# Low-weight products of the two-row weight pieces, issued singly behind 512-column products instead of in runs

## The reference, cut to what matters

```python
x = x + jnp.square(jax.nn.relu(hf @ ffn_w1[layer])) @ ffn_w2[layer]       # hidden width 4096, two layers
...
return (jax.nn.silu(h @ w_gate) * (h @ w_up)) @ w_down                     # swiglu, hidden width 2816
```

## Time and profile before

| | us |
|---|---|
| median of 3 runs (lowest, highest) | 874.14 (873.94, 874.26) |
| the profiled execution, device time | 874.67 |
| its span, first to last instruction | 872.9 |
| TensorE busy in the span | 864.1 (99%) |
| DVE busy | 622.4 (71%) |
| ACT busy | 452.9 (52%) |

### The profile page before, as it was taken

How to read it: one execution, slowest core, us unless ns; L and a number is a source line. 1 busy time by engine, 2 the same in 40 slices (tenths; PEclk the granted TensorE clock), 3 DMA queues, 4 the chain that set the end, 5 groups by cost and what they waited for, 6 DMA issues and landing times.

```text
span 872.9 us, 12188 instructions
## 1 busy us (share of the span) xinstructions
PE 864.1 (99%) x4714; PEld 739.8 (85%) x4714; DVE 622.4 (71%) x783; ACT 452.9 (52%) x619; POOL 80.9 (9%) x115
## 2 busy tenths in 40 slices
PE   9999999999999999999999999999999999999997
PEld 8988888888888988778888888888877888888886
DVE  6899877766666678857666666667775876676675
ACT  5697554433434578745343444465775844434432
POOL 3484110000000020011000000020000200000000
PEclk9999999999999999999999999999999999999999
DMA  9665356565555362376655555556442456555541
GB/s 303 213 215 193 112 179 219 169 212 192 187 189 193 116 191 86 106 250 204 207 192 190 190 191 193 188 182 200 145 146 97 140 178 213 193 191 193 192 145 48
DMA packets 98393, 155.84 MB, mean 179 GB/s; under 512 B 4144, under 2 KB 73421, under 8 KB 98349
## 3 DMA queue, kind: packets, MB, share of 16 engines
q1 hardware_dynamic: 95644, 149.37, 51.0%
q0 software_dynamic: 1648, 5.80, 2.2%
q10 hardware_dynamic: 1056, 0.07, 0.1%
HBM read 153.62 MB, written 1.09 MB: 177 GB/s over the span
## 4 chain that ended last, share of the span: by engine, by line
PE 98%; DMA 1%; DVE 0%; ACT 0%; issue 0%; SPq 0%; DVEq 0%; POOLq 0%; POOL 0%; ACTq 0%
PE psum L2090 21%; PE psum L1984 16%; PE psum L1985 16%; PE psum L1986 16%; PE psum L2096 11%; PE psum L2076 4%; PE psum L2079 2%; PE psum L2591 1%; PE psum L2622 1%; PE psum L2005 1%; PE psum L2268 1%; PE psum L2604 1%; PE psum L2043 1%; PE psum L2048 1%; PE psum L2044 1%; PE psum L2702 1%
## 5 line engine op out<-in xcount | busy, mean ns | idle before, releaser
L1297 DVE TENSOR_TENSOR w_lo<-raw,w_hi 128x2048 fp32r<-128x2048 f32 (+3 forms) x116 | 259.6, 2247 | 79.9 <-ACT w_hi L793 39.1
L2090 PE MATMUL psum<-h_both,w_hi 128*128 128x512 f32 x800 | 190.0, 389 | 0.0
L2090 PEld LDWEIGHTS psum<-h_both,w_hi 128*128 128x128 f32 x800 | 149.3, 188 | 30.4
L775 ACT ACTIVATE w_hi<-raw 128x2048 fp32r<-128x2048 f32 (+2 forms) x71 | 129.6, 1838 | 36.6 <-PE psum L1986 23.6
L1984 PE MATMUL psum<-w_hi,g_hi 128*128 128x512 f32 x368 | 144.6, 393 | 0.0
L1985 PE MATMUL psum<-w_lo,g_hi 128*128 128x512 f32 x368 | 143.7, 390 | 0.0
L1986 PE MATMUL psum<-w_hi,g_lo 128*128 128x512 f32 x368 | 143.3, 389 | 0.0
L793 ACT ACTIVATE w_hi<-raw 128x2048 fp32r<-128x2048 f32 x66 | 125.7, 1911 | 23.9 <-PE psum L1986 23.9
L2096 PEld LDWEIGHTS psum<-h_both,w_lo 128*128 128x128 f32 x800 | 102.7, 191 | 4.0
L968 ACT ACTIVATE g_hi<-g_mul 128x512 fp32r<-128x512 f32 x32 | 20.3, 634 | 162.7 <-DVE g_mul L1612 162.7
L2096 PE MATMUL psum<-h_both,w_lo 128*128 128x256 f32 x800 | 103.9, 283 | 0.0
(11 more groups left out here) (312 smaller groups left out, 1098.5 us busy)
## 6 DMA issues: line engine op xcount, KB each, us to landing
raw<-in_ffn_w SPq DMA_DIRECT2D x64, 1024.0 KB, 5.3
raw<-in_w_qkv SPq DMA_DIRECT2D x12, 1024.0 KB, 5.1
raw<-in_ab_w_in SPq DMA_DIRECT2D x11, 1024.0 KB, 6.5
raw<-in_w_gate SPq DMA_DIRECT2D x11, 1024.0 KB, 5.3
raw<-in_w_up SPq DMA_DIRECT2D x11, 1024.0 KB, 5.4
raw<-in_w_down SPq DMA_DIRECT2D x11, 1024.0 KB, 5.7
raw<-in_ab_w_out SPq DMA_DIRECT2D x4, 1024.0 KB, 4.9
raw<-in_c_w_out SPq DMA_DIRECT2D x4, 1024.0 KB, 6.5
```

Source lines behind the costliest of these rows:

```text
L775: ins = act.activation(dst, src, ACT.Copy)
L1297: ins = dve.tensor_tensor(dst, src, high, ALU.subtract)
L2090: pe.matmul(bank(b + f), wh[:, k, f * P:(f + 1) * P], h_both[:, k, :, :].rearrange("p u s -> p (u s)"), start=k == 0, stop=False, skip_gro ...
```

## The change

Two functions are new, and the last-row handling of `stationary_both` moves into what follows it.

- `stationary_open` does high(0), with the low products of row 1 of an earlier piece between them where one is given, and then high(1) with low(0) between: one 512-column product, one 256-column product, and so on. It leaves its own low(1) open.
- `out_closing` does the 24 products of `out_piece` and puts the 8 open low products of the piece before behind the first 8 of them; the last of the 8 increments `piece_used` for that piece.
- In `ffn`, each first-matrix piece is `stationary_open` and the second-matrix piece after it `out_closing` (15 chunks in each of the two networks). In the gated network, up closes gate and down closes up (9 chunks). The last gate and up pieces stay with `stationary_both`, whose low(0) now also goes between the products of high(1) for the gate piece.

The numbers and sizes of all products, and DVE's, ACT's and SP's programs, are the same.

The helpers `high_at` and `low_at` issue one product of `high` and `low` each. The diff's core:

```diff
                 else:
-                    high(1)
-                    low(0)
+                    for k in range(KB):
+                        high_at(slot, b, 1, k)
+                        low_at(slot, b, 0, k)
                 low(1).then_inc(piece_used, 1)
+
+            def stationary_open(slot, b, slot_before=None, b_before=None):
+
+                for k in range(KB):
+                    high_at(slot, b, 0, k)
+                    if slot_before is not None:
+                        ins = low_at(slot_before, b_before, 1, k)
+                if slot_before is not None:
+                    ins.then_inc(piece_used, 1)
+                for k in range(KB):
+                    high_at(slot, b, 1, k)
+                    low_at(slot, b, 0, k)
+
+            def out_closing(act_of, n_slot, first, slot_before, b_before):
...
+                            for term, (a, w) in enumerate(((a_hi, wh), (a_hi, wl), (a_lo, wh))):
+                                ins = pe.matmul(bank(2 * tb + h), a, w[:, k, cs], start=first and k == 0 and term == 0,
+                                                stop=False)
+                                if left < KB:
+                                    low = low_at(slot_before, b_before, 1, left)
+                                    left += 1
+                                    if left == KB:
+                                        low.then_inc(piece_used, 1)
+                ins.then_inc(piece_used, 1)
...
-                    stationary_both(n % RING, hidden_banks(j + 1))
+                    stationary_open(n % RING, hidden_banks(j + 1))
...
-                    out_piece(hidden_of(j % 3), (n + 1) % RING, isinstance(c, int) and c == 0)
+                    out_closing(hidden_of(j % 3), (n + 1) % RING, isinstance(c, int) and c == 0,
+                                n % RING, hidden_banks(j + 1))
...
+                    stationary_open(n0 % RING, 4)
+                    split(n0 + 1 + 6 * i)
+                    pe.wait_ge(mul_out, hb + c)
+                    stationary_open((n0 + 1) % RING, 6, n0 % RING, 4)
...
-                out_piece(glu_of(j % 2), (n + 2) % RING, isinstance(c, int) and c == 0)
+                out_closing(glu_of(j % 2), (n + 2) % RING, isinstance(c, int) and c == 0, (n + 1) % RING, 6)
```

More of the change, by code:

```diff
@@ L2081, in stationary_half, with high_at, low_at @@
                 return ins
+            def high_at(slot, b, f, k):
+                wh = w_hi[:, slot, :].rearrange("p (k c) -> p k c", k=KB)
+                return pe.matmul(bank(b + f), wh[:, k, f * P:(f + 1) * P],
+                                 h_both[:, k, :, :].rearrange("p u s -> p (u s)"),
+                                 start=k == 0, stop=False, skip_group_check=True)
+            def low_at(slot, b, f, k):
+                wl = w_lo[:, slot, :].rearrange("p (k c) -> p k c", k=KB)
+                return pe.matmul(bank(b + f)[:, 0:S], wl[:, k, f * P:(f + 1) * P], h_hi[:, k, :],
+                                 start=False, stop=k == KB - 1, skip_group_check=True)
             def stationary_both(slot, b, half_done=None):
-                wh = w_hi[:, slot, :].rearrange("p (k c) -> p k c", k=KB)
-                wl = w_lo[:, slot, :].rearrange("p (k c) -> p k c", k=KB)
                 def high(f):
                     for k in range(KB):
-                        pe.matmul(bank(b + f), wh[:, k, f * P:(f + 1) * P],
-                                  h_both[:, k, :, :].rearrange("p u s -> p (u s)"),
-                                  start=k == 0, stop=False, skip_group_check=True)
+                        high_at(slot, b, f, k)
                 def low(f):
                     for k in range(KB):
-                        ins = pe.matmul(bank(b + f)[:, 0:S], wl[:, k, f * P:(f + 1) * P], h_hi[:, k, :],
-                                        start=False, stop=k == KB - 1, skip_group_check=True)
+                        ins = low_at(slot, b, f, k)
                     return ins
@@ L2104, in stationary_both @@
                 else:
-                    high(1)
-                    low(0)
+                    for k in range(KB):
+                        high_at(slot, b, 1, k)
+                        low_at(slot, b, 0, k)
                 low(1).then_inc(piece_used, 1)
+            def stationary_open(slot, b, slot_before=None, b_before=None):
[9 more added lines that the diff above has]
+            def out_closing(act_of, n_slot, first, slot_before, b_before):
+                wh = w_hi[:, n_slot, :].rearrange("p (k c) -> p k c", k=2)
+                wl = w_lo[:, n_slot, :].rearrange("p (k c) -> p k c", k=2)
+                left = 0
+                for tb in range(TB):
+                    for h in range(2):
+                        cs = slice(h * 512, (h + 1) * 512)
+                        for k in range(2):
+                            a_hi, a_lo = act_of(k, tb)
+                            for term, (a, w) in enumerate(((a_hi, wh), (a_hi, wl), (a_lo, wh))):
[7 more added lines that the diff above has]
+                ins.then_inc(piece_used, 1)
             def stationary_seam(slot, t, b, x_at):
@@ L2858, in gate_up @@
                     pe.wait_ge(gate_scaled, c)
[L2859 to L2862, removed]
+                if isinstance(c, int) and c == GC - 1:
+                    stationary_both(n0 % RING, 4)
+                    split(n0 + 1 + 6 * i)
+                    pe.wait_ge(mul_out, hb + c)
+                    stationary_both((n0 + 1) % RING, 6, up_half)
+                else:
+                    stationary_open(n0 % RING, 4)
+                    split(n0 + 1 + 6 * i)
+                    pe.wait_ge(mul_out, hb + c)
+                    stationary_open((n0 + 1) % RING, 6, n0 % RING, 4)
             def glu_of(r):
```

## The result

| | before | changed |
|---|---|---|
| median, us | 874.35 (873.94 to 875.08, 6 runs) | 882.23 (882.08 to 882.93, 6 runs) |
| span of the profiled execution, us | 872.9 | 880.3 |
| TensorE busy in it | 864.1 | 869.9 |

The changed kernel takes 1.009 times as long, 95% interval 1.008 to 1.010: 7.9 us slower, where 4.3 were forecast; 882.23 lies above the forecast's range, which ended at 881.2. All that follows reads the two traces, whose spans differ by 7.4 us.

A forecast was written before the change was run, and what follows sets the result against it. TensorE, busy 99% of the span, was taken to bound the kernel. Product distances +1.4, two seams +3.0 and the gated network 0 gave +4.4 us; forecast 878.4 us, range 873.6 to 881.2.

The forecast's parts named there:

- the price of a pair: TensorE, one 256-column product behind one 512-column product, repeated: +2 ns each time, 776 times, 1.55 us.
- the products' own part: TensorE's product distances: 1.55 us for alternating sizes, less 0.18 for fewer run exits in gated chunks, +1.4 us.
- The equal 13.3 ns: TensorE: 512- and 256-column products each pay 13.3 ns besides their columns, so no load time is left to hide.
- The two stretches of the earlier trace: TensorE, 384 and 288 columns in turn, two pairs each: 0.62 and 0.63 us against 0.613, +3 to +8 ns a pair.
- The upper bound of 8 ns: TensorE, worst pair of 384 and 288 columns, taken as the most a 512-256 pair could add: +8 ns.
- Seams: After each network's last chunk, DVE's read-out comes 1.82 us later and TensorE's transposes wait: 1.5 us each, +3.0 us.
- The loops: Network and gated chunks: DVE's read-outs come 1.82 us later, yet weights reach TensorE in time; 0 us counted.
- Gaining pairs (1 and 2): TensorE, low behind high cheaper: 6 to 7 ns gained, 873.4 us, chance 0.15; or 9 ns, 872.2, chance 0.05.
- An unstalled seam (3): After each network's last chunk, unseen slack prevents the stall: 875.5 us, or 874.0 with flat pairs; chance 0.12.
- DVE's loop (4): Gated network: DVE's chain to the next up weights binds, each chunk 0.1 to 0.3 longer, 879.5 to 881.5; chance 0.12.
- Pairs at the upper bound (5): TensorE, each high-low pair costs +8 ns: 883.1 us; chance 0.04.
- The signs written down for a wrong forecast: TensorE's timeline: pairs at 0.34 us or less, transposes following at once, or idle before second-matrix or up pieces.

The follow-up runs named there:

- experiment 6: Changed kernel with each low product taking 512 columns instead of 256, so sizes no longer alternate but weights and banks do: 961.79 us.
- experiment 7: Kernel before with each low product right behind its own high one, same bank, lows widened to 384 columns, then 496: 920.77 and 952.11 us.
- experiment 3: Kernel before with row 1's 8 lows in one run behind the second matrix's first 8 products, all 15 chunks of each network: 878.14 us.
- experiments 1 and 2: Changed kernel, each network's last first-matrix piece closing itself: 879.78 us; kernel before, last chunks' 8 row-1 lows put behind 8 second-matrix products: 877.33 us.
- experiment 5: Kernel before with the bank changing at every product while the sizes stay in runs of 16 highs, then 16 lows: 874.39 us.

## Why the prediction was wrong

**The step that failed is the price of a pair,** the 2 ns in "What does one low behind one high cost, repeated?". It measured 6.7 ns: 776 x 6.7 = 5.2 us in place of 1.55. With the exits, the products' own part came to 5.0 us where 1.4 was forecast; the 0.18 that the gated chunks were to gain by one exit less did not come. The equal 13.3 ns of long and short products was read rightly, and nothing speaks against the conclusion that no load time is there to be hidden: in experiment 6 the loads still come from `w_hi` and `w_lo` in turn, at no cost, and in experiment 7 a low that gives a load more time is no cheaper. The mistake came behind it. The two stretches of the earlier trace rows gave +3 and +8 ns as they are printed, and the value taken lay below both, for a reason (the mixed sizes around them) for which there was no row. Their middle, 5.5, would have given 881.2, the upper end of the range. But the rows themselves could not have given 6.7: to the nanosecond they are 616 and 624 ns, +1.3 and +5.3 a pair, and each holds only two pairs, less than the three after which the pattern of 512 and 256 repeats. The upper bound of 8 ns held by the rounding of the rows, a piece of luck; a chance of 0.04 was all that it got, and so the range ended below it.

**Seams: right, a little large.** 2.5 us in place of 3.0. The chain was the one described, each step behind the other. Its 0.5 us too much hid a part of the pairs' miss in the total. The error is in the last step: the estimate compared the loads, 291.95 against 290.36, 1.6. Before, the first product stood 0.23 behind its load; in the stalled kernel both start at 293.08, 0.06 behind the residual's end. By the products the same estimate is 291.98 - 290.59 = 1.4, and the residual began 0.08 before the end that its forerunner's row shows, where 0.03 behind it was assumed: 1.3.

**The loops: right.** DVE's L1608 waits 2.2 us, not 3.1, since the second piece of its `w_lo` now follows the first at once and ends later; TensorE waits nowhere in the networks, as experiment 3 shows without pairs. In the gated network TensorE stayed ahead of DVE's loop, by little. The first of DVE's two `w_lo` here is done at about 789.3, and the product that waits for it, up's first, starts 0.4 later:

```profile
787.00 4.49 DVE L1312 TENSOR_TENSOR w_lo<-raw,w_hi 128x2048 fp32r<-128x2048 f32 x2 [1.11 <-ACT w_hi L793]
789.65 0.40 PE L2086 MATMUL psum<-h_both,w_hi 128*128 128x512 f32 x1
```

This was partly luck. The forecast's 16.62 us for TensorE alone takes 122 ns a low where the earlier trace rows give 120; with 120 and flat pairs it is 16.55, no longer than the 16.56 of the loop. It was the pairs' extra 0.2 us a chunk that kept TensorE clear of it. What flat pairs would have given was not run.

**Rivals.** Gaining pairs (1 and 2): refuted, the 113 ns behind a high is paid back by the next high. An unstalled seam (3): refuted by the trace and experiments 1 and 2. DVE's loop (4): not reached. Pairs at the upper bound (5) is nearest to what happened, with 6.7 of its 8 ns. The signs written down for a wrong forecast were a pair at 0.34 us or less, transposes at once, and idle time: none of them would show a pair that is too dear. The chunk times do, 11.11 and 16.79 us against 11.05 and 16.7 at most. The Trainium skill, "TensorE: Matmul & The Clock Gate", section "Back-to-back issue gap", gives N / 2.4 + 2.5 ns for a lone product and says that in a stream the load and the product set the spacing together. The formula was no guide here: distances were N / 2.4 + 13.3 in runs of 256 and of 512 columns (120.0 and 226.7 ns), and more for 256 or 384 with 512 in turn.

## What to carry to other kernels

On an engine that is busy 99% of the time a new order of its instructions must be priced by distances from start to start of the very pattern that it makes, over whole periods: the first short distance behind a long product was 113 ns, and the period still grew. Where only near rows exist, keep their whole spread in the range, and treat even that as rough when they hold only a pair or two: here two pairs of 384 and 288 columns gave +1.3 and +5.3 ns, and the pattern to be priced cost 6.7. And when the end of a piece is put off inside a loop with slack, look at the last iteration by itself: what follows it may hang on a chain that has none.

## What was not expected of the hardware

- Products of 512 columns with 256- or 384-column ones singly in turn cost 6.7 ns a pair over N / 2.4 + 13.3 each; with 496-column ones nothing. With 256 columns the pattern of starts has a period of three pairs.
- A run of 4 to 16 short products costs 20 to 22 ns once. Behind a run of 8 or 16 the cost is spread over five long products (233, 236, 228, 232, 231 ns in place of 226.7), less 7 at the run's first short one. Runs of two cost 3 each. Why the cost is not monotonic in the length, and what inside TensorE makes it, stays open: no run here shows it.
- The bank may change with every product at no cost (experiment 5: a chunk of 11.01 us, as before), and so may the tile that the weights come from, at 512 columns (experiment 6: 226.7 ns).
